# A decoder trunk on one core: the weight halves of the unit two ahead, made before the modulation work of the step instead of after it

## What is computed

```python
cond = jax.nn.silu(c)
for l in range(DEPTH):                                   # DEPTH = 2
    mod = cond @ w_mod[l] + b_mod[l]                     # 2048 x 12288 weights for one row
    sh1, sc1, g1, sh2, sc2, g2 = jnp.split(mod, 6, axis=-1)
    h = modulate(rms_norm(x, norm_gain[l, 0]), sh1, sc1)
    y = attention_mixer(...) if l % 2 == 0 else pool_mixer(...)
    x = x + g1[:, None, :] * y
    h = modulate(rms_norm(x, norm_gain[l, 1]), sh2, sc2)
    x = x + g2[:, None, :] * conv_ffn(h, w_up[l], conv_w[l], conv_b[l], w_down[l])
return rms_norm(x, final_gain)
```

## Time and profile before

| what | value |
|---|---|
| median of 3 runs | 2180.98 us (2180.72 to 2181.45) |
| time of the profiled execution | 2182.51 us |
| its span | 2180.9 us |
| PE busy | 2056.4 us (94%) |
| DVE busy | 1651.0 us (76%) |
| ACT busy | 1060.5 us (49%) |
| read from HBM | 552.14 MB |
| granted TensorE clock, mean | 0.977 |

### The profile page before, as it was taken

One profiled execution on the slowest core, in us unless ns is written; L12 is line 12 of the kernel. 1 busy time (PEld: TensorE's weight loads), 2 busy tenths in 40 slices (PEclk: granted clock), 3 DMA queues, 4 the chain that ended last, 5 costly groups with the idle time before them and its releaser, 6 DMA issues.

```text
span 2180.9 us, 39430 instructions
## 1 busy us (share of the span) xinstructions
PE 2056.4 (94%) x14034; PEld 1915.5 (88%) x14034; DVE 1651.0 (76%) x2286; ACT 1060.5 (49%) x1392; POOL 309.1 (14%) x459
## 2 busy tenths in 40 slices
PE   2689999999899999999999999899989999999998
PEld 2679998987899978999789987699978999889996
DVE  5887888889878898887987886787855565655665
ACT  3327564454556544445444545555543454434553
POOL 3332222224311121111221110011100000000000
PEclk9789999999999999999999999999999999999999
DMA  8988999988677799777997784288745555555552
GB/s 286 359 312 289 360 327 329 333 311 301 235 279 263 247 363 336 262 282 263 329 346 273 265 288 137 83 291 282 250 136 193 192 171 190 182 194 188 177 188 97
DMA packets 235510, 555.50 MB, mean 255 GB/s; under 512 B 13993, under 2 KB 15001, under 8 KB 235161
## 3 DMA queue, kind: packets, MB, share of 16 engines
q1 hardware_dynamic: 180120, 352.93, 47.3%
q0 software_dynamic: 55296, 201.35, 25.5%
HBM read 552.14 MB, written 2.10 MB: 254 GB/s over the span
## 4 chain that ended last, share of the span: by engine, by line
PE 78%; DVE 8%; DMA 6%; issue 4%; ACT 2%; DVEq 0%; ACTq 0%; POOLq 0%; POOL 0%
PE ps L507 18%; PE ps L509 18%; PE ps L508 18%; PE ps L532 7%; PE ps L534 7%; PE ps L533 7%; DMA mraw<-in_w_mod 6%; DVE w_lo L1134 3%; DVE macc L1148 3%; PE ps L550 1%; ACT work L847 1%; ACT w_hi L847 1%; PE ps L578 0%; PE ps L560 0%; ACT macc L847 0%
## 5 line engine op out<-in xcount | busy, mean ns | idle before, releaser
L1134 DVE TENSOR_TENSOR w_lo<-raw,w_hi 128x1024 fp32r<-128x1024 f32 x664 | 800.0, 1223 | 406.0 <-ACT w_hi L847 400.7
L847 ACT ACTIVATE w_hi<-raw 128x1024 fp32r<-128x1024 f32 x664 | 693.3, 1056 | 836.5 <-PE ps L509 528.2
L507 PE MATMUL ps<-h_hi,w_hi 128*128 128x256 f32 x3328 | 951.2, 286 | 27.7 <-DVE w_lo L1134 25.7
L508 PE MATMUL ps<-h_lo,w_hi 128*128 128x256 f32 x3328 | 946.6, 284 | 0.0
L509 PE MATMUL ps<-h_hi,w_lo 128*128 128x256 f32 x3328 | 946.4, 284 | 0.0
L507 PEld LDWEIGHTS ps<-h_hi,w_hi 128*128 128x128 f32 x3328 | 644.0, 194 | 29.7 <-issue 26.2
L508 PEld LDWEIGHTS ps<-h_lo,w_hi 128*128 128x128 f32 x3328 | 644.3, 194 | 0.1
L509 PEld LDWEIGHTS ps<-h_hi,w_lo 128*128 128x128 f32 x3328 | 643.7, 193 | 0.0
L1148 DVE SCALAR_TENSOR_TENSOR macc<-mraw,cond,macc 128x512 f32<-128x512 f32 x636 | 438.2, 747 | 50.8 <-DMA mraw<-in_w_mod 45.6
L415 POOL DMA_DIRECT2D mraw<-in_w_mod x366 | 265.1, 725 | 1247.9 <-DVE macc L1148 771.5
L532 PE MATMUL ps<-w_hi,g_hi 128*128 128x512 f32 x832 | 327.0, 393 | 7.8 <-DVE w_lo L1134 7.5
(11 more groups left out here) (146 smaller groups left out, 1101.5 us busy)
## 6 DMA issues: line engine op xcount, KB each, us to landing
mraw<-in_w_mod POOLq DMA_DIRECT2D x366, 512.0 KB, 6.2
raw<-in_w_up SPq DMA_DIRECT2D x176, 1024.0 KB, 5.1
raw<-in_w_down SPq DMA_DIRECT2D x88, 1024.0 KB, 5.1
raw<-in_w_attn_in SPq DMA_DIRECT2D x48, 1024.0 KB, 8.0
raw<-in_w_attn_out SPq DMA_DIRECT2D x16, 1024.0 KB, 7.3
work<-in_w_mod POOLq DMA_DIRECT2D x12, 512.0 KB, 7.7
raw<-in_w_pool SPq DMA_DIRECT2D x4, 1024.0 KB, 5.3
pmat<-in_w_mod POOLq DMA_DIRECT2D x6, 512.0 KB, 9.5
```

The costliest lines, as they stand in the source:

```text
L507: mm(o, wh, ah, start=st, stop=False, skip_group_check=True)
L508: mm(o, wh, al, start=False, stop=False, skip_group_check=True)
L847: return nc.scalar.activation(o, i, f, **kw)
L1134: V.tensor_tensor(w_lo[:, s, :, :], raw[:, j % 4, h * 1024:(h + 1) * 1024].rearrange("p (k n) -> p k n", k=2), w_hi[:, s, :, :].bitcast(F3 ...
```

## The change

Only the order of calls inside a step changes, on ScalarE and VectorE, at nine places: the attention and output steps, the up-projection loops, the down-projection loops and the last down-projection. `split` of the unit two ahead comes first, and then the step's `first_products` on ScalarE and its `piece` calls on VectorE. TensorE's, SyncE's and GpSimd's programs are the same.

```diff
--- before.py
+++ after.py
@@ -996,11 +996,11 @@
                         gate_copy(0, cg)
                     act.wait_ge(consts, C_ONES)
                     sqrt_table()
+                if pos < 63:
+                    split((pos + 2) // 4, (pos + 2) % 4)
                 for ch, j in mod_at(pos):
                     if j == 0:
                         first_products(ch, (ch + 1) % 2, ch - 1)
-                if pos < 63:
-                    split((pos + 2) // 4, (pos + 2) % 4)
                 g = qkv_done(pos)
                 if g is not None:
                     hg, kind, _ks = qkv_unit(pos)
@@ -1050,9 +1050,9 @@
                         for half in range(2):
                             for ks in range(4):
                                 j = 4 * half + ks
+                                split(q + 2 * i, j + 2)
                                 if with_mod and j == 1:
                                     first_products(i + ch, 0, i + ch)
-                                split(q + 2 * i, j + 2)
                                 if ks == 3:
                                     conv_last_tap(l, 8 * q + 16 * i + 8 * (half + 1), (ya, yg)[half],
                                                   4 * i + (4 * g0 + FT * half), half,
@@ -1086,10 +1086,10 @@
                     else:
                         sqrt_table()
                         for u in range(12):
+                            if u < 11 and 4 * q + u + 2 < UNITS:
+                                split(q + (u + 2) // 4, (u + 2) % 4)
                             if l == 0 and u == 0:
                                 first_products(ch, 0, ch)
-                            if u < 11 and 4 * q + u + 2 < UNITS:
-                                split(q + (u + 2) // 4, (u + 2) % 4)
                             if u in (2, 5, 8):
                                 squares(2 * l + 2, u // 3)
                         if l == 0:
@@ -1455,9 +1455,6 @@
                         for u in range(12):
                             if l == 0 and u == 5:
                                 mod_bias(ch, 1, ch - 24)
-                            if l == 0 and u < 4:
-                                for p in (2 * u, 2 * u + 1):
-                                    piece(ch, p, 0)
                             if l == 0 and u == 8:
                                 dve.wait_ge(mod_ready, 24 + 12)
                                 V.tensor_tensor(gps[:, :], mods[:, 96 + G1:96 + G1 + KT], prm[:, PSC:PSC + KT],
@@ -1465,6 +1462,9 @@
                                 norm_gain_vec(2)
                             if u < 11 and 4 * q + u + 2 < UNITS:
                                 split(q + (u + 2) // 4, (u + 2) % 4)
+                            if l == 0 and u < 4:
+                                for p in (2 * u, 2 * u + 1):
+                                    piece(ch, p, 0)
                             if u % 3 == 2:
                                 cg = u // 3
                                 residual(g + cg, 8 * q + 2 * u + 2, cg % 2, grow_mlp, 512 * cg, gates, before + 2 * cg)
```

## The result

| | before | after |
|---|---|---|
| median of 4 runs each, us | 2181.22 (2180.72 to 2183.44) | 2260.13 (2257.54 to 2262.59) |
| ratio with 95% interval | 1 | 1.0361 (1.0344 to 1.0377) |
| profiled execution, us | 2182.51 | 2257.54 |
| its span, us | 2180.9 | 2255.9 |
| granted TensorE clock, mean | 0.977 | 0.962 |

The changed kernel is 3.6% slower: 78.9 us between the medians, 75.0 between the two spans. The forecast was 2231 us; the time lies at the high end of the range, 0.13 us above it.

What follows compares the result with a forecast made beforehand. TensorE was taken to bound all of it, with VectorE and DMA close behind in the down-projection. Terms 15.7 + 5.3 + 16.2 + 3.1 + 13.6 = +53.9 us, taken as 50, gave 2231 us; range 2202 to 2260.

Steps and rivals of the forecast that it cites:

- feed-forward of layer 0, waits: Late modulation sums: 0.35 us in each of 11 up-projection iterations, +16.2 in two down-projection loops, +3.1 in the last down-projection.
- attention and output, waits: Attention and output projection: sums come late, +7.3 us at chunk 16, +4.4 at chunk 21, +4 at others, together +15.7.
- taken off for overlap: Whole kernel: waits counted apart overlap in places, so the sum of +53.9 us was taken as 50.
- The up-projection's 0.35: Up-projection loops: each iteration's sum comes 0.35 us late (0.2 to 0.5); 15 iterations make +5.3 us.
- the rival of the clock falling behind the sums: Down-projection loops: the clock falls behind every sum, six more falls costing 20 us, time 2251; chance 0.2.
- price of 3.4 for a fall: Each clock fall costs 0.9 us for the sum and 2.5 behind it; four falls make +13.6 us (0 to 13.6).
- The transfer: Down-projection loops: piece 7's load, 7.5 us from piece 3, puts the sum at 25.85; 25.2 taken, +2.0 per chunk.
- The floor of the prediction: Down-projection loops: VectorE's chain alone puts the next sum 24.55 us after L1152, 1.35 above the earlier 23.2.
- +7.3 for chunk 16: Attention: pieces 3 to 5 behind their split push back the softmax bias, so chunk 16's sum is 7.3 us later.
- +4.4 for chunk 21: Output projection: pieces delay residual, squares and halves at position 54, so L1152 ends at 504.6, +4.4 us.
- +4 for the other chunks: Output projection: chunks 18, 19, 22 and 23 come 0.6 to 2.2 us late, taken as +4 (0 to 5.6).
- What it said would show: Traces: L550 waits 40 us or more, `w_lo` waits nearly vanish, down-projection sums 25 us apart, waits of 4 us or more.

Runs made afterwards that it cites:

- e3_down_only: New order only in the two down-projection loops of layer 0, otherwise the kernel before: 2208.69 us, ratio 1.0128.
- e1_att_only: New order only in the attention and output steps (positions 9 to 63), otherwise the kernel before: 2218.12 us, ratio 1.0169.
- e7_around_all: Kernel before, with the split's first half ahead of the modulation work and second half behind, in feed-forward loops and attention: 2218.21 us, ratio 1.0168.

## Why the prediction came out as it did

The direction and the mechanism were right: pieces and halves cost what they did, the sums wait for L1152, and waits for low halves nearly vanish. The size was 50 us where the profiles differ by 75. By its own terms:

| term | predicted us | measured us (idle or busy time of TensorE) |
|---|---|---|
| feed-forward of layer 0, waits (11 x 0.35 + 16.2 + 3.1) | 23.2 | 22.4 |
| the same, clock (three new falls) | 10.2 | 12.6 (six new falls) |
| attention and output, waits | 15.7 | 25.7 |
| the same, clock (one new fall) | 3.4 | 13.3 (six new falls) |
| layer 1 (4 x 0.35) | 1.4 | 1.0 (all outside the two stretches) |
| taken off for overlap | -3.9 | none seen: the four places add up |

**Feed-forward: 33.4 predicted, 35.0 measured.** That it is so near is in part luck. By the starts of the sums the two down-projection loops cost 14.5 + 12.1 = 26.6 us for 16.2 + 6.8 = 23.0, the up-projections 5.0 for 3.9, and the last down-projection 3.5 for 3.1 + 3.4 = 6.5. The up-projection's 0.35 was 0.44 per iteration, inside its bounds. In all of this stretch the sums' waits grew from 2.5 to 29.9 us, +27.4 for the 23.2, and the 4.3 us in which products waited for low halves went the other way, which the terms hardly counted. The sums of the first down-projection loop came 27.4 us apart and not 25.2. Of the excess of 4.6 over TensorE's own 22.8, the waits are 2.3 on average (3.07, 2.09, 1.67), which is the forecast's 2.4. The rest is the clock, which fell behind the short waits too (0.72 in the 6 us from 847 and from 874, and 0.75 in `e3_down_only` behind 1.77 us of waiting). So the rival of the clock falling behind the sums was half right: of its six shorter waits three had a fall behind them (3.07, 2.09 and 2.50 us) and three had none (1.67, 1.74 and 1.64). The argument against it, that short waits of before had no fall behind them, did not hold for waits of 2 to 3 us; those of before in these loops were under 1 us. Its price of 3.4 for a fall was too high for these: at 0.72 over 6 us one costs 1.7, the three together 5 us and not the rival's 20. This is the place where the Trainium skill, "TensorE: Matmul & The Clock Gate", section "HAM oscillation — how this bites in real kernels", was weighed: it tells of a clock that falls anew in every iteration with a wait. The trace now agrees in part: the clock fell at three sums of the four in the first loop, and at two of four in the second.

**The transfer** played next to no part. In the chunk shown, piece 7 waited 0.32 us for its load at 898.03; GpSimd had issued it at 892.00, 6.0 us before, where the earlier trace rows had 6.9. The DMA engines had more room, at a share of 0.84 from 818 to 900 us instead of 0.99. The floor of the prediction, 24.55 us, was the chain that counts.

**Attention: this step failed.** It was the term of 15.7 us: +7.3 for chunk 16, +4.4 for chunk 21, +4 for the other chunks. It asked only which modulation *sums* come late. The pieces between the split and the next step also stand ahead of the head's own work on VectorE, and TensorE waits for that, or for a bias (L1158) behind it, at L665 and L647, which no term held. These waits are 7.2 + 4.9 + 1.9 = 14.0 us in five places, none of them there before. The sums' own waits in this stretch grew from 5.0 to 46.0 - 29.9 = 16.1, so by 11.1 for the 15.7, and with 14.0 that is the +25.7 but for 0.6 (3.8 us of other new waits and 2.6 of waits for halves that are gone nearly cancel). The size shows it too, by how much later than before a sum starts, clock included: 11.4 us had come together by chunk 15 (366.46, before 355.05), with waits of 1.89 us at 223.54 and 4.18 at 304.22, both at L665, and the prediction had nothing there; 9.7 came with chunk 16, for its 7.3; and 18.4 from there to chunk 23, for 4.4 + 4 and 3.4 of the clock. The prediction had seen for chunk 16 that the softmax bias is pushed back, and priced it for the sum behind it, not for the matmul L647 that waits for the same L1302. The clock went the same way: one fall was counted, behind chunk 23, and chunk 21's was taken as free; there were falls at L665 (0.57 in the 4 us from 224 and in the 8 us from 302), at L647 (0.50 in the 6 us from 477), at L647 and chunk 16 (0.57 over 20 us from 382), and behind chunks 21 to 23. `e1_att_only` and `e7_around_all` show that this is the attention's alone, and that sending only half of the split ahead helps it little. That the waits of the head matmuls for VectorE's pieces are the reason is read from the rows; no run takes the pieces out from between.

**What it said would show** came true for the waits of L550 (46.0, expected 40 or more), the waits for halves, position 39, the wait at about 1300 us (5.04 at 1373.48), and layer 1 behind its fourth iteration, which takes within 1 us of its time before. At about 500 us the expected wait of 4 us was one of 1.60 at 533.33, with a wait of 2.2 for the residual L1229 that ended at 526: the pieces held up the residual itself.

## What to carry to other kernels

In an in-order queue, work that is ready belongs ahead of an instruction that waits for the bottleneck engine, not behind it. Putting it behind turns the waiting time, which was free, into lateness. When such work is moved, price every consumer of every instruction that now stands behind it, not only the consumer of the moved result: here the attention, where this was left out, was about half of the cost. And if a late result has to be lived with, move the place where the bottleneck asks for it: one unit later gave back 20.7 us, while the same move in a kernel whose sums were in time gave nothing.

## What the runs showed of the hardware

The granted clock fell behind waits as short as 1.6 to 2.1 us. The eight small matmuls of a sum need not follow: behind 1.89 us of waiting at 223.54, followed by two matmuls of a head, it was 0.57 in the 4 us from 224. The length of the wait alone did not decide it: behind 1.67 us at 900.22 the clock stayed at 1.00 for the next 10 us, behind 1.60 us at 533.33 it was 0.83 on average; behind 2.10 us at 832.12 in `e3_down_only` it was 1.00 in the 6 us from 832, behind 2.09 us at 873.99 in the changed kernel 0.72. What decides it instead, no run here takes apart. Over the same work, 185 to 1460 us before and 185 to 1535 after, TensorE's clock was at the 1.2 GHz level for 23.9 us before and 95.6 after.

```profile
533.33 1.05 PE L550 MATMUL ps<-ones,macc 128*128 128x1 f32 x8 [1.60 <-DVE macc L1152]
```

```profile
533.00:543.00 10.00, 9.67 (x40) 7.97 (x41) 8.26 (x13) 5.35 (x8) 2.18 (x3) 0.83 0.72 264
```
